# First pass of a hybrid decoder step: other order of the first loads, a spare weight block, setup slots ended at activations, tables started later

## What is computed

```
y = y + 0.5 * (silu(n1(y) @ wg1) * (n1(y) @ wu1)) @ wd1          # feed-forward 1, 1024 -> 2816 -> 1024
q, k, v, u = split(n2(y) @ w_in)
attn = sliding_window_attention(q, k, v, rel_bias, sinks)        # window 128
ssm  = s5(u, state; lam_bar = exp(lam*dt), b_bar, C, d_skip)     # 32 groups x 64 complex states, then GELU and GLU
y = y + concat(attn, ssm) @ w_out
y = y + 0.5 * (silu(n3(y) @ wg2) * (n3(y) @ wu2)) @ wd2          # feed-forward 2
return n4(y), caches, states                                     # n1..n4 are RMSNorms
```

## Time and profile before

| what | value |
|---|---|
| runs shown | 1339.89, 1455.2 and 1494.41 us, median 1455.2 |
| profiled execution | 1338.18 us |
| its spans, 8 cores | 1319.4 to 1336.6 us, slowest core 0 |
| TensorE (PE) busy on core 0 | 1241.2 us, 93% |
| VectorE (DVE), ScalarE (ACT), GpSimd (POOL) busy | 667.6, 393.2, 126.9 us |
| chain that ended last | PE 77%, DVE 8%, DMA 5%, issue 4%, ACT 3% |
| mean DMA rate | 88 GB/s |

### The profile page before, as it was taken

One profiled execution on the slowest core, in us unless ns is written; L12 is line 12 of the kernel. 1 busy time (PEld: TensorE's weight loads), 2 busy tenths in 40 slices (PEclk: granted clock), 3 DMA queues, 4 the chain that ended last, 5 costly groups with the idle time before them and its releaser, 6 DMA issues.

```text
span 1336.6 us, 21400 instructions; the slowest of 8 cores (1319.4 to 1336.6 us)
## 1 busy us (share of the span) xinstructions
PE 1241.2 (93%) x7695; PEld 666.2 (50%) x7774; DVE 667.6 (50%) x1357; ACT 393.2 (29%) x686; POOL 126.9 (9%) x210
## 2 busy tenths in 40 slices
PE   4698899998999999999989899999999979999997
PEld 1243344444566446665546544334445545666665
DVE  2355765354178537844362266568834543232226
ACT  2343411533212432223342213432234431101123
POOL 2011120011000000000120000000010000110000
PEclk9898999999999999999999999999999989999999
DMA  9356644358244324434492243334455249464323
GB/s 216 63 115 185 147 84 80 60 78 103 37 103 79 60 41 93 86 65 66 62 126 37 58 90 65 59 76 86 83 82 95 33 105 193 74 115 80 64 33 135
DMA packets 62263, 117.35 MB, mean 88 GB/s; under 512 B 24072, under 2 KB 30632, under 8 KB 61872
## 3 DMA queue, kind: packets, MB, share of 16 engines
q0 software_dynamic: 43632, 80.79, 38.2%
q1 hardware_dynamic: 18528, 35.18, 8.5%
HBM read 183.39 MB, written 15.37 MB: 149 GB/s over the span
## 4 chain that ended last, share of the span: by engine, by line
PE 77%; DVE 8%; DMA 5%; issue 4%; ACT 3%; SPq 1%; DVEq 0%; ACTq 0%; POOLq 0%
PE ps L205 69%; PE psy L205 9%; DMA wf<-wgu 3%; ACT rt_s L209 2%; SPq L83 1%; DVE hA_s L215 1%; DMA scr_tab<-hB_s 1%; ACT L209 1%; DVE hA_s L212 1%; DVE xT_s L215 1%; DVE mix_s L212 1%; DVE hB_s L212 1%; DVE aT_s L212 1%; ACT sg_s L209 1%; DMA xT_s<-xT 1%
## 5 line engine op out<-in xcount | busy, mean ns | idle before, releaser
L205 PE MATMUL ps<-hB_s,wf 128*128 128x384 bf16 (+1 forms) x2112 | 334.8, 320 | 11.5 <-DVE aT_s L212 4.7
L205 PE MATMUL ps<-hA_s,wf 128*128 128x512 bf16 x1370 | 320.6, 392 | 26.3 <-DMA wf<-wgu 9.8
L205 PE MATMUL ps<-aT_s,wf 128*128 128x512 bf16 (+4 forms) x1611 | 303.5, 343 | 10.5 <-DVE xT_s L215 6.4
L209 ACT ACTIVATE sg_s<-ps 128x512 f32<-128x512 f32 (+3 forms) x284 | 147.8, 537 | 548.5 <-PE ps L205 468.6
L212 DVE TENSOR_TENSOR aT_s<-ps,sg_s 128x512 bf16<-128x512 f32 (+2 forms) x220 | 129.9, 595 | 336.6 <-PE ps L205 243.9
L205 PEld LDWEIGHTS ps<-hB_s,wf 128*128 128x128 bf16 x2112 | 207.2, 99 | 136.1 <-issue 20.1
L205 PEld LDWEIGHTS ps<-hA_s,wf 128*128 128x128 bf16 x1408 | 139.7, 100 | 201.5 <-issue 51.3
L205 PEld LDWEIGHTS ps<-aT_s,wf 128*128 128x128 bf16 x1628 | 154.8, 98 | 152.7 <-issue 28.7
L215 DVE SCALAR_TENSOR_TENSOR xT_s<-ps,xT_s 128x384 f32<-128x384 f32 (+4 forms) x188 | 108.1, 576 | 177.7 <-PE ps L205 177.1
L83 POOL DMA_DIRECT2D wf<-wgu x88 | 47.2, 537 | 688.5 <-PE ps L205 653.1
L209 ACT ACT_TABLE_LOAD x37 | 47.5, 1283 | 91.3 <-PE ps L205 59.6
(11 more groups left out here) (177 smaller groups left out, 836.4 us busy)
## 6 DMA issues: line engine op xcount, KB each, us to landing
wf<-wgu POOLq DMA_DIRECT2D x88, 512.0 KB, 5.4
wf<-wd POOLq DMA_DIRECT2D x59, 352.0 KB, 4.4
scr_tab<-hB_s SPq DMA_DIRECT2D x8, 512.0 KB, 6.8
hA_s<-scr_tab SPq DMA_DIRECT2D x16, 256.0 KB, 3.8
hB_s<-scr_tab SPq DMA_DIRECT2D x16, 256.0 KB, 4.1
yT<-xT_s SPq DMA_DIRECT2D x8, 512.0 KB, 7.5
xT_s<-xT SPq DMA_DIRECT2D x4, 768.0 KB, 5.8
wm_s<-wout POOLq DMA_DIRECT2D x12, 256.0 KB, 3.7
```

The lines of the kernel that those rows point to most:

```text
L205: return self.P.op('pe', lambda e: e.matmul(out, lhsT, rhs, start=start, stop=stop, skip_group_check=skip), waits=waits, signal=signal)
L209: return self.P.op('act', lambda e: e.activation(out=out, in_=in_, func=func, **kw), waits=waits)
```

## The change

It does five things in the first pass. Block 0 of the weights is issued with no wait, and tile 1 of the tokens waits for its landing too. A fourth block is loaded into the mixer's `wm_s` once tile 1 has landed; its release frees the mixer's buffers and issues no load. SP waits for tile 1 before the setup loads. In `setup_gen` a slot ends before and after the activations of `lam` and after the one for `ES`, and the Exp for `rho4` moves up beside the other one. The tables begin in the fifth slot from the one that sets `t_tp`.

```
--- before.py
+++ after.py
@@ -138,6 +138,7 @@
         self.items = items
         self.nxt = 0
         self.ready = []
+        self.spare = None
 
     def issue(self, waits=()):
         if self.nxt < len(self.items):
@@ -145,10 +146,21 @@
             self.nxt += 1
             self.ready.append(self.ring.load(src, n, waits))
 
+    def issue_spare(self, ring, dst, slot, waits):
+
+        src, n = self.items[self.nxt]
+        self.nxt += 1
+        self.spare = ring
+        self.ready.append((dst, ring.P.dma('pool', dst, src, slot, waits=waits), None))
+
     def take(self):
         return self.ready.pop(0)
 
     def release(self, i, tok):
+        if i is None:
+            for k in range(len(self.spare.bufs)):
+                self.spare.release(k, tok)
+            return
         self.ring.release(i, tok)
         self.issue()
 
@@ -365,11 +377,13 @@
         for p in range(4):
             tx.append(self.load_x(0, 2 * p, 2))
         self.feed = Feed(self.fring, self.weight_order())
-        self.feed.issue(waits=[tx[0]])
+        self.feed.issue()
         self.feed.issue(waits=[tx[1]])
         for p in range(2):
-            self.load_x(1, 4 * p, 4, [tx[3]])
+            self.load_x(1, 4 * p, 4, [tx[3], self.feed.ready[0][1]])
         self.feed.issue(waits=[self.tok_x[(0, 1)]])
+        self.feed.issue_spare(self.mring, self.wm[:, :], self.slot("d_spare"), [self.tok_x[(4, 1)]])
+        P.wait_only('sp', [self.tok_x[(4, 1)]])
         sgen = self.setup_gen()
         next(sgen)
 
@@ -379,6 +393,7 @@
         setup = Stream(sgen, 0.75)
         tabs = Stream(self.tabs_gen(), 0.5)
         nrm = Stream(self.norm_first_b(), 0.8)
+        tp_slots = 0
         for st, h, us in self.ffn(0, 0, pre={1: lambda: self.norm_now(0, 1, 7)}):
             self.slot_no += 1
             if self.slot_no % 5 == 0 and xrest:
@@ -388,7 +403,9 @@
             if not setup.done:
                 setup.pump(us)
             if self.t_tp is not None and not tabs.done:
-                tabs.pump(us)
+                tp_slots += 1
+                if tp_slots > 4:
+                    tabs.pump(us)
             if setup.done and tabs.done:
                 nrm.pump(us)
         setup.drain()
@@ -1383,19 +1400,25 @@
 
 
         def lam(aR, aI, ldt, T, is_pm, extra=()):
+            yield None
             yield va(ldt, ldt, AF.Exp, extra) or c
             yield vtt(T['xr'], aR, ldt, ALU.mult) or c
             yield vtt(T['xi'], aI, ldt, ALU.mult) or c
+            yield None
             yield va(T['mag'], T['xr'], AF.Exp) or c
+            if is_pm:
+                yield va(pm['rho4'], T['xr'], AF.Exp, scale=4.0) or c
+            yield None
             yield vts(T['xi'], T['xi'], 1.0 / TWO_PI, None, ALU.mult) or c
             if is_pm:
                 yield vcp(pm['turns'], T['xi']) or c
-                yield va(pm['rho4'], T['xr'], AF.Exp, scale=4.0) or c
             yield vcp(T['ni'], T['xi']) or c
             yield vcp(T['nf'], T['ni']) or c
             yield vtt(T['xi'], T['xi'], T['nf'], ALU.subtract) or c
+            yield None
             yield va(T['s1'], T['xi'], AF.Sin, scale=TWO_PI) or c
             yield va(T['sh'], T['xi'], AF.Sin, scale=float(np.pi)) or c
+            yield None
             yield vtt(T['sh'], T['sh'], T['sh'], ALU.mult) or c
             yield vts(T['sh'], T['sh'], -2.0, 1.0, ALU.mult, ALU.add) or c
             yield vtt(T['L1r'], T['mag'], T['sh'], ALU.mult) or c
```

1 line of the change is left out of this document (removed).

## The result

The changed kernel took 1319.36 us, the median of four executions (1317.94 to 1322.46); four executions of the kernel before, taken beside it, took 1332.80 to 1494.41 us. The ratio of the two is 0.9873, with a 95% interval of 0.9856 to 0.9890: 1.3% faster. The forecast was 1319.0.

What follows compares the result with a forecast made beforehand. TensorE was taken as the bound, with nearly all its holes in the first feed-forward pass. Gains of 23.9 us on core 0 (1312.7) and 14.6 on core 7 (1317.4, slowest) plus 1.6 gave 1319.0; range 1304 to 1332.

Steps and rivals of the forecast that it cites:

- the fourth block: Near 57 us: wait of 6.53 us (core 7: 6.78) and slow matmuls (2.81, 2.85) go; fifth block just in time.
- It removes nothing: Setup activations on ScalarE: silus now between them, two table loads of 1.28 us added; counted nothing, bounds 0 and 2.6.
- The later tables: ScalarE's table-store wait goes, 8.89 us on core 0 only; 2.61 us down-stage hole goes, 3.99 (core 7: 4.35).
- the 0.5 us given back in the down stage: Six of eight tables lie there, their POOL multiplies in front of weight loads: 0.5 us lost, 0 to 3.
- the prediction's own signs: Trace signs of right or wrong; wrong at the tables if TensorE waits for wd blocks or ScalarE in first down stage.
- nothing is counted there: Past the first pass all engines keep their order apart from ring buffer numbers, so no gain or loss was counted.
- The second sum: Gains on core 7, taken as slowest apart from core 0: 14.6 us, giving 1317.4 and making it the slowest.
- About what a measurement of this kernel can tell from no change: Said of a 2% difference when setting chances: 0.24 faster by over 2%, 0.03 slower, 0.73 within.
- the first rival: Core 7's slower rest is chance and core 0's gain comes in full, 26.6 us: 1311.6 or a little under; chance 0.25.
- First loads: First real matmul 2.2 us later, but its pair's other 31 start sooner: 1.0 us gained core 0, 0.5 core 7.
- The third rival: Weights first make tokens late, and block 1 too: a loss of 2 us instead of the gain, 1321.5; chance 0.12.
- The 0.5 us for the norm behind the pass: Other token half's last 16 multiplies, 8.3 us of VectorE, fall behind the pass: 0.5 us lost, 0 to 2.

Runs made afterwards that it cites:

- e2: Kernel before with only the first loads reordered (weight block 0 unwaited, tile 1 behind it, setup loads behind tile 1): 1339.62 us, ratio 1.0010.
- e8: Changed kernel with the first loads put back in the order of before: 1318.64 us, ratio 0.9855 to the kernel before.
- e1: Kernel before with only the spare fourth weight block added: 1332.02 us, ratio 0.9941.
- e3: Kernel before with only the setup slots ended at the activations and the Exp for rho4 moved: 1331.57 us, ratio 0.9940.
- e11: Changed kernel without the new ends of setup slots: 1328.10 us, ratio 0.9927 to the kernel before.
- e4: Kernel before with only the tables begun four slots later: 1336.01 us, ratio 0.9980.
- e9: Changed kernel with the tables begun at once, four slots sooner: lowest 1320.44 us, ratio 0.9876 to the kernel before.
- e5: Changed kernel with the six token loads of half B issued behind the first down stage: 1317.24 us, ratio 0.9829 to the kernel before.
- the last experiment: Changed kernel with later half-B tokens, split tile 1 norm and the last pass's two cache copies 20 slots later in the program: 1313.85 us, ratio 0.9823.

## Why the prediction was right, and which steps failed

The forecast of 1319.0 us met the measured 1319.36, and the mechanism of the fourth block held. Three steps of the working failed. The setup slots, of which the prediction said "It removes nothing" and which it counted at nothing, give 0.60% alone, as much as the spare block. The later tables, to which it gave 8.89 + 3.99 us on core 0, give 0.20% alone. And the 0.5 us given back in the down stage was 4.29 us of waiting and 2.8 of slow clock on the slowest core. By the prediction's own signs it was wrong at the tables, since TensorE waits for `wd` blocks in the first down stage on seven cores. In the chances it failed as well: a gain of this size was called hardly measurable, and it is clear of the noise.

**The sum.** The end of the first pass came 23.4 us sooner on core 0 (297.2 to 273.85), where 23.9 were summed up, and 16.7 sooner on core 7 (288.4 to 271.67), where it was 14.6. That the slowest core met the forecast is in part luck. Core 7 came out 3.2 us shorter than forecast (1314.2 against 1317.4). In the profiled execution core 2, which neither sum looked at, was the slowest, by a wait that the sum had at 0.5 us and by a rest of the program 6.2 us longer than in the kernel before; that execution took 1322.46, and the median of four is 1319.36. That "nothing is counted there", past the first pass, came out by two differences that cancel: the wait for a weight block at the start of the second pass (0.9 to 2.75 us on six cores before) is gone, and the one near 1100 us grew from 2.6 to 4.9 us in the mean of the cores, so that the rest takes 1039.8 us before and 1039.9 after.

**The second sum.** Core 7 was taken as the slowest apart from core 0; core 3 was longer by 0.2 us (1332.2 against 1332.0), and its hole at the start of the down stage was 5.87 us, a size that neither sum has.

**"About what a measurement of this kernel can tell from no change."** This step failed in the weighing of chances. The intervals above reach 0.12 to 0.27% to either side, about a tenth of the 2% that the text gave, so a gain of 1.3% is told from none with ease. The forecast of 1.4% below the profiled execution was itself a forecast of a clear gain. The 0.24 for under 1311.4 us does not follow either: the first rival, which it leans on, was summed up to 1311.6, "or a little under".

**First loads.** The mechanism was right: the first matmul comes at 18.9 to 20.3 us, with no hole of note in the pair. Its worth is nothing that e2 and e8 can measure, where 1.0 and 0.5 us were put. The third rival's loss did not come either.

**Fourth block.** This was right, with the fifth block in time by the 0.4 us forecast on core 0. On its own the spare block gave 0.6% (e1), 8 us.

**"It removes nothing", of the setup slots.** This was wrong. e3 gives 0.6% by this part alone, and e11, which takes it out of the change, loses most. The 2.61 us hole and the VectorE holes were put under the later tables; e4 leaves the 2.61 us hole where it was, e3 removes it. What the prediction said removes it (no exp with its table loads in front of the last silu) fits the traces, but the exp moves because the setup is cut at its activations and so ends later. The cost was rightly put at nothing: the table loads show as no hole.

**Tables later.** It was right that the store wait in front of the last silus goes (e4, and e9, in which it returns in the down stage), and wrong in what it is worth: 5.92 + 2.97 us on core 0 was one draw. In the kernel before, TensorE had it on one core with that size; in e1 on four, with 2.8 to 5.3 us; in e2 on four, two of them others, with 2.3 to 5.0. Alone the part is worth 0.2%.

**"Given back: 0.5 (0 to 3)" for weight loads behind multiplies on POOL.** The place was right, the mechanism wrong and the size too small. POOL issues in time; the loads land late while tokens of half B, beside the table stores, take the DMA engines, and with the tokens moved away the wait goes (e5). It costs 0.5 to 4.3 us by draw, with 2.8 of slow clock at the long one. The 0.5 us for the norm behind the pass wasn't needed: the 8.01 us of multiplies end at 281.66, the next product follows at once, and TensorE has no bracket there, although the wait for weights that was to cover part of it (2.04 us on core 7) is gone.

**The slow clock at the start of the down stage.** It was counted beside the VectorE hole that follows, but the two trade off. In the kernel before, the 11 matmuls behind the 2.61 us hole took 3.81 us on core 0 with a VectorE hole of 1.09 behind them, and 4.13 on core 7 with one of 0.77: 4.90 us on both.

**Do the parts add up?** They do within the noise: 0.59 + 0.60 + 0.20 - 0.10 = 1.29% for the four alone, 1.27% for the change and 1.51% when it was run again, with 0.1 to 0.3% of uncertainty on each.

## What to carry to other kernels

With eight cores the slowest counts, so a wait that strikes some core or other costs about its largest draw, and it has to be looked for on all cores and in a second execution, not on the slowest of one profile. When side work is moved out of one stage, write down what its transfers will meet in the next: here moving six loads of tokens out of the stage that had inherited the tables removed the new wait on all cores. Cutting side work at its long-latency steps, so that the main engine's own instructions stand between them, was worth as much here as removing a 6 us wait for a load (0.60 and 0.59%). And when an order is changed to test a cause, look in the trace whether the instruction moved in time: the copies of the last experiment did not.

## What the runs showed of the hardware that was not expected

The same hole can cost a slow clock or not. On core 1 of the kernel before a hole of 3.71 us precedes the stretch from 60 us on, on core 1 of e2 one of 3.68; the stretch ran at clock 0.76 in the one and at 1.00 in the other (columns as in the earlier trace rows):

```profile
60.00:72.00 12.00, 11.54 (x42) 4.79 (x43) 5.64 (x26) 1.69 (x4) 0.53 (x1) 0.76 0.53 75
```

```profile
60.00:72.00 12.00, 11.76 (x54) 5.11 (x55) 5.97 (x28) 3.57 (x6) 0.53 (x1) 1.00 0.73 109
```

In the 29 matmuls from about 44 us, before that hole, the first had taken 8.55 us and the second 8.08. So two holes of one length had different prices in clock, and the 2.8 us that the forecast added per long hole are shown only for the cores it was read from.

A slow clock in front of another wait cost nothing: in e1, after the 2.61 us hole, 11 matmuls took 4.22 us on core 1 with a VectorE wait of 0.69 behind, and 2.54 us on core 2 with one of 3.07 behind, so that the next group came no sooner at full clock.

Issuing can take as long as the transfer: four bias loads hold SP for 5.0 to 14.5 us over the cores and runs, and a table store waits behind them. On core 0 of the kernel before it was 13.56 us, and the largest of the four landed 11.8 us after its issue. The Trainium skill, DMA: Bandwidth & Descriptors, "Issuing engines are not separate DMA queues", calls the time to initiate a DMA usually small relative to the DMA itself. For these four loads it is not.
